# Activations in alternating 64-byte pieces for a float32r transformer kernel on one core

## The chip, the cores and the metric

The kernel runs on one core of one Trainium2 chip. The metric is the device time of one execution in microseconds (us), the median of several executions. A difference of 0.2% (3.5 us) is about what a measurement of this kernel can tell from no change.

## The reference, cut to what matters

Ten sublayers work on one sequence of 256 tokens with 1024 channels. Each normalizes the residual stream, scales and shifts it by values computed from a conditioning vector, runs a mixer or a feed-forward network, and adds the result back through a gate:

```
def modulate(x, g, c_act, w, b):
    m = c_act @ w + b
    shift, scale, gate = jnp.split(m, 3, axis=-1)
    h = rmsnorm(x, g) * (1.0 + scale[:, None, :]) + shift[:, None, :]
    return h, gate[:, None, :]

def swiglu(h, w_gate, w_up, w_down):
    return (jax.nn.silu(h @ w_gate) * (h @ w_up)) @ w_down
```

In the order of the kernel the sublayers are: feed-forward, Mamba-2 mixer, feed-forward, feed-forward, block attention ("moba"), feed-forward, stick-breaking attention ("sb"), convolutional feed-forward, sparse latent attention ("dsa"), convolutional feed-forward. The feed-forward width is 2816. Everything is float32.

## The kernel before, in words

**Layout.** Activations lie transposed: channels on the 128 partitions, the 256 tokens (T) along the free axis. The normalized input of a stage is eight such tiles (KT = 8, index kk).

**Three products for one.** Float32 accuracy comes from float32r products (F32R). Every operand is split into a high part (a rounded copy, made by ScalarE) and a low part (the rest, made by VectorE as original minus copy). `three` (lines 1573 to 1577) then issues hi x hi, hi x lo and lo x hi, each a 128x128 stationary weight tile under a 128x256 moving activation tile. Weights come in 276 blocks of 128x2048, one megabyte each, by SP's queue into `raw` (six buffers). ScalarE writes `w_hi` (line 496), VectorE `w_lo` (line 915), three buffers each, two blocks ahead of TensorE (AHEAD = 2). One block is 48 products.

**Activations.** `norm` builds a stage's input. VectorE writes the scaled tiles (`t`, line 1036), ScalarE adds the shift and rounds into `h_hi` (line 530), VectorE writes the low part (line 1043). TensorE's first block of a stage (`gemm` with `first`) takes the tiles as they come: 32 products with `h_hi` (lines 1588, 1591), then 16 with the low parts (line 1602), each pair waiting for its tile. Later blocks of a stage run over kk = 0 to 7 for each half of the block. The products of a feed-forward's down projection and of the mixers' output projections (`gemm_out`, `last`, `early_out`) read `a_hi` and `a_lo`, which ScalarE (lines 555, 603, 684, 749) and VectorE (lines 1120, 1176, 1293, 1414) write once per group. In the attention stages some blocks ("tokens") have it the other way about: activations stationary and weights moving.

**Addresses.** `h_hi` lies 1472 bytes behind a multiple of 8192 bytes from the weight buffers (x, `folded3`, `gs` between them), `h_lo_rest` (tiles 1 to 7) directly behind it, so both begin 192 bytes past a multiple of 256 from the weights. Tile 0 of the low part has a buffer of its own, `h_lo_first`, 64 bytes further on, a multiple of 256 from the weights. For kk = 0 the low product is issued first (lines 1632 to 1634, in place of `three`).

```
        h_hi = sb("h_hi", [P, KT, T], F32R)
        h_lo_rest = sb("h_lo_rest", [P, KT - 1, T], F32R)
        gap = sb("gap", [P, 16])
        h_lo_first = sb("h_lo_first", [P, T], F32R)
        gap2 = sb("gap2", [P, 48])
```

**Order.** Each engine runs its own list in order; semaphores tie them. VectorE's list carries side work too: in stages 0, 2, 3, 5 and 7 it accumulates the modulation vectors of later stages (line 970, from `modws`), spread over the iterations by a table. In a stage's `norm` it stands as eight `t`, eight low parts, then the rest of a weight split (`late_split`). During a `norm` TensorE runs filler products on the first weight block (`fill`, line 1697), moving and stationary operand both from `w_hi`.

## Time and profile before

| | |
|---|---|
| median of 3 runs | 1773.77 us (1773.60 to 1774.51) |
| the profiled execution | 1783.76 us, span 1782.0 us |
| TensorE matmul busy | 1742.4 us (98%), 14686 products |
| VectorE busy | 1452.5 us (82%) |
| ScalarE busy | 956.5 us (54%) |
| mean granted TensorE clock | 0.998 of full speed |

Matmuls are pipelined, so that one recorded product overlaps the next two. The busy share says little; the distance from start to start is what a product costs. It is read from the timeline or as a window's length over its count.

### The profile page before, as it was taken

Reading aid. Unit: us, or ns where it says so; the run is one execution under the profiler, and the core shown is the slowest. Engines: PE = TensorE matmul, PEld = TensorE weight load, DVE = VectorE, ACT = ScalarE, POOL = GpSimd, SP = SyncE. Lnnn points to the kernel's source line nnn. Section 1 sums busy time; section 2 is a strip of 40 time slices with the busy share of each in tenths; the row PEclk is TensorE's granted clock in tenths of the full one; section 3 lists DMA queues with packets and bytes.
Section 4 is the critical chain, followed back from the end, with each engine's and each line's share of the span. In section 5 each row is a group of like instructions: output and inputs, shape, how many; then the busy total and the mean of one; then the engine's idle time right before and its main releaser. Section 6 shows DMA issues by size and latency. Waiting matters only on the chain.

```text
span 1782.0 us, 34261 instructions
## 1 busy us (share of the span) xinstructions
PE 1742.4 (98%) x14686; PEld 1699.3 (95%) x14686; DVE 1452.5 (82%) x1750; ACT 956.5 (54%) x1254; POOL 0.2 (0%) x4
## 2 busy tenths in 40 slices
PE   5999999999999999999999999999999999999999
PEld 4999999998999999999999999999999998989999
DVE  7799899988898879897558989765899888567776
ACT  4444566676533454445765333566655556675553
POOL 0000000000000000000000000000000000000000
PEclk9999999999999999999999999999999999999999
DMA  9999734443798859895436988343387545316550
GB/s 395 411 420 332 308 143 166 166 144 141 313 394 328 331 204 389 326 379 183 149 141 227 387 309 352 147 154 124 127 302 282 210 147 187 141 72 218 186 199 34
DMA packets 68149, 426.23 MB, mean 239 GB/s; under 512 B 7488, under 2 KB 10832, under 8 KB 31824
## 3 DMA queue, kind: packets, MB, share of 16 engines
q1 hardware_dynamic: 63936, 416.22, 61.3%
q10 hardware_dynamic: 4112, 8.62, 1.4%
q8 instruction: 68, 1.11, 0.3%
q14 instruction: 33, 0.27, 0.0%
HBM read 423.74 MB, written 3.17 MB: 240 GB/s over the span
## 4 chain that ended last, share of the span: by engine, by line
PE 93%; DVE 3%; ACT 3%; DMA 1%; issue 0%; DVEq 0%; SPq 0%; ACTq 0%
PE bank L1575 25%; PE bank L1576 24%; PE bank L1577 24%; PE bank L1632 2%; PE bank L1634 2%; PE bank L1633 2%; PE bank L1588 1%; PE bank L1688 1%; PE bank L1602 1%; PE bank L1991 1%; DMA mix<-mods 1%; PE bank L1591 1%; ACT w_hi L496 1%; PE bank L1859 1%; ACT work L719 0%; PE bank L1972 0%
## 5 line engine op out<-in xcount | busy, mean ns | idle before, releaser
L1575 PE MATMUL bank<-h_hi,w_hi 128*128 128x256 f32 x2504 | 696.2, 278 | 0.0
L1577 PE MATMUL bank<-h_hi,w_lo 128*128 128x256 f32 x2504 | 695.2, 278 | 0.0
L1576 PE MATMUL bank<-h_lo_rest,w_hi 128*128 128x256 f32 x2504 | 695.2, 278 | 0.0
L915 DVE TENSOR_TENSOR w_lo<-raw,w_hi 128x2048 fp32r<-128x2048 f32 x267 | 609.5, 2284 | 91.4 <-ACT w_hi L496 90.4
L496 ACT ACTIVATE w_hi<-raw 128x2048 fp32r<-128x2048 f32 x276 | 527.9, 1913 | 159.7 <-PE bank L1577 146.1
L1575 PEld LDWEIGHTS bank<-h_hi,w_hi 128*128 128x128 f32 x2504 | 473.0, 189 | 0.0
L1576 PEld LDWEIGHTS bank<-h_lo_rest,w_hi 128*128 128x128 f32 x2504 | 470.2, 188 | 0.0
L1577 PEld LDWEIGHTS bank<-h_hi,w_lo 128*128 128x128 f32 x2504 | 470.1, 188 | 0.0
L1575 PE MATMUL bank<-a_hi,w_hi 128*128 128x256 f32 x1280 | 358.6, 280 | 0.8 <-DVE a_lo L1293 0.8
L1577 PE MATMUL bank<-a_hi,w_lo 128*128 128x256 f32 x1280 | 355.4, 278 | 0.0
L1576 PE MATMUL bank<-a_lo,w_hi 128*128 128x256 f32 x1280 | 355.4, 278 | 0.0
L1575 PEld LDWEIGHTS bank<-a_hi,w_hi 128*128 128x128 f32 x1280 | 241.9, 189 | 3.1 <-issue 1.4
L1576 PEld LDWEIGHTS bank<-a_lo,w_hi 128*128 128x128 f32 x1280 | 240.4, 188 | 0.1
L1577 PEld LDWEIGHTS bank<-a_hi,w_lo 128*128 128x128 f32 x1280 | 240.4, 188 | 0.0
L970 DVE SCALAR_TENSOR_TENSOR macc<-modws,cact,macc 128x1536 f32<-128x1536 f32 x126 | 225.8, 1811 | 1.2 <-DMA modws<-mods 1.2
L1156 DVE SCALAR_TENSOR_TENSOR mix<-bank,par,mix 128x254 f32<-128x254 f32 (+1 forms) x176 | 76.7, 477 | 41.3 <-ACT mix L582 39.8
L1632 PE MATMUL bank<-h_lo_first,w_hi 128*128 128x256 f32 x344 | 100.2, 291 | 1.6 <-DVE work L1378 1.4
L555 ACT ACTIVATE a_hi<-mix 128x512 fp32r<-128x512 f32 x40 | 25.3, 633 | 141.0 <-PE bank L1577 125.5
L1634 PE MATMUL bank<-h_hi,w_lo 128*128 128x256 f32 x344 | 97.8, 284 | 0.0
L1633 PE MATMUL bank<-h_hi,w_hi 128*128 128x256 f32 x344 | 96.6, 281 | 0.0
L582 ACT ACTIVATE mix<-bank,par 128x256 f32<-128x256 f32 x88 | 44.9, 561 | 91.8 <-PE bank L1577 91.8
L541 ACT ACTIVATE mix<-bank 128x512 f32<-128x512 f32 x44 | 26.4, 600 | 117.8 <-PE bank L1577 117.7
(304 smaller groups left out, 1986.3 us busy)
## 6 DMA issues: line engine op xcount, KB each, us to landing
raw<-weights SPq DMA_DIRECT2D x276, 1024.0 KB, 5.3
modws<-mods SPq DMA_DIRECT2D x144, 768.0 KB, 6.7
mix<-mods SPq DMA_DIRECT2D x5, 1024.0 KB, 8.8
mix<-mods ACTq DMA_DIRECT2D x8, 512.0 KB, 13.3
biases<-scratch ACTq DMA_DIRECT2D x1, 2048.0 KB, 13.3
mix<-biases ACTq DMA_DIRECT2D x4, 512.0 KB, 3.8
modws<-mods SPq DMA_DIRECT2D x1, 1024.0 KB, 11.6
x<-xin SPq DMA_DIRECT2D x1, 1024.0 KB, 10.9
```

Of the source, the lines that this page charges most:

```text
L496: eng.activation(w_hi[g % NW][:, :], raw[g % NRAW][:, :], ACT.Copy).then_inc(sems["whi"], 1)
L541: k.inc("silu", eng.activation(sg, bank[4][:, :].rearrange("p (a t) -> p a t", a=2), ACT.Silu))
L582: ins = eng.activation(dst[:, m, :], b[:, m * T:(m + 1) * T], ACT.Identity, scale=cw(i, t, 2), bias=cw(i, t, 3))
L915: eng.tensor_tensor(w_lo[g % NW][:, :], raw[g % NRAW][:, :], w_hi[g % NW][:, :], ALU.subtract).then_inc(sems["wlo"], 1)
L970: ins = eng.scalar_tensor_tensor(out=m, in0=modw[q % 4], scalar=c, in1=m, op0=ALU.mult, op1=ALU.add)
L1156: ins = eng.scalar_tensor_tensor(out=dst[:, m, lag:T], in0=b[:, m * T:(m + 1) * T - lag], scalar=cw(i, 22 * up + m, tap), in1=dst[:, m, la ...
L1575: eng.matmul(dst, ah, bh, start=start, stop=False, skip_group_check=skip)
L1576: eng.matmul(dst, ah, bl, start=False, stop=False, skip_group_check=skip)
L1577: return eng.matmul(dst, al, bh, start=False, stop=stop, skip_group_check=skip)
L1632: eng.matmul(d, hi[:, kk, part], h_lo(kk), start=True, stop=False)
L1633: eng.matmul(d, hi[:, kk, part], h_hi[:, kk, :], start=False, stop=False)
L1634: eng.matmul(d, lo[:, kk, part], h_hi[:, kk, :], start=False, stop=False)
```

## The change

`h_hi`, `h_lo_all` (all eight low tiles in one buffer), `a_hi` and `a_lo` now begin 128 bytes past a multiple of 256 bytes from the weight buffers, by gaps of other sizes. `h_lo_first` and the low-product-first order for kk = 0 are gone; `three` serves all kk. Except for `h` in the stages moba and sb, a tile of 256 tokens is stored as two halves of 512 bytes: tokens 0 to 15 in the first, 16 to 31 in the second, 32 to 47 in the first, and so on. The moving operand of each product is an access pattern that takes 64 bytes (16 tokens) from one half, then 64 from the other, so that the product sees the tokens in order. ScalarE writes `h_hi` in this order by one instruction with a longer pattern. The writes of `a_hi` on ScalarE and of all low parts on VectorE become two instructions each, one per half. In moba and sb `h` is stored in token order, since blocks there use it as the stationary operand.

```diff
+        gap = sb("gap", [P, 48])
         h_hi = sb("h_hi", [P, KT, T], F32R)
-        h_lo_rest = sb("h_lo_rest", [P, KT - 1, T], F32R)
-        gap = sb("gap", [P, 16])
-        h_lo_first = sb("h_lo_first", [P, T], F32R)
-        gap2 = sb("gap2", [P, 48])
+        h_lo_all = sb("h_lo_all", [P, KT, T], F32R)
+        gap2 = sb("gap2", [P, 16])
+        def by_chunks(tile):
+            return tile.rearrange("p (e j q) -> p j e q", e=2, q=16)
+        def in_order(tile):
+            return tile.rearrange("p (j e q) -> p j e q", e=2, q=16)
+        def chunked(st):
+            return stages[st] not in ("moba", "sb")
+        def h_lo(n, st):
+            return by_chunks(h_lo_all[:, n, :]) if chunked(st) else in_order(h_lo_all[:, n, :])
+        def hh(n, st):
+            return by_chunks(h_hi[:, n, :]) if chunked(st) else in_order(h_hi[:, n, :])
...
+        gap3 = sb("gap3", [P, 48])
         a_hi = sb("a_hi", [P, 2, T], F32R)
         a_lo = sb("a_lo", [P, 2, T], F32R)
+        def halves(tiles, e):
+            return tiles[:, :, e * P:(e + 1) * P].rearrange("p a (j q) -> p a j q", q=16)
+        def halves_in_order(tiles, e):
+            return tiles.rearrange("p a (j e q) -> p a j e q", e=2, q=16)[:, :, :, e]
...
-                    k.inc("hhi", eng.activation(h_hi[:, m, :], work3[:, m, :], ACT.Identity,
+                    k.inc("hhi", eng.activation(hh(m, st), in_order(work3[:, m, :]), ACT.Identity,
                                                 bias=modv[:, st, m:m + 1]))
...
-                    k.inc("ahi", eng.activation(z_hi if final else a_hi[:, :, :], act, ACT.Copy))
+                    to = z_hi if final else a_hi
+                    for e in range(2):
+                        ins = eng.activation(halves(to, e), halves_in_order(act, e), ACT.Copy)
+                    k.inc("ahi", ins)
...
-                    k.inc("hlo", eng.scalar_tensor_tensor(
-                        out=h_lo(m), in0=work3[:, m, :], scalar=modv[:, st, m:m + 1],
-                        in1=h_hi[:, m, :], op0=ALU.add, op1=ALU.subtract))
+                    for e in range(2):
+                        ins = eng.scalar_tensor_tensor(
+                            out=h_lo(m, st)[:, :, e], in0=in_order(work3[:, m, :])[:, :, e], scalar=modv[:, st, m:m + 1],
+                            in1=hh(m, st)[:, :, e], op0=ALU.add, op1=ALU.subtract)
+                    k.inc("hlo", ins)
...
-                    k.inc("alo", eng.tensor_tensor(z_lo if final else a_lo[:, :, :], act,
-                                                   z_hi if final else a_hi[:, :, :], ALU.subtract))
+                    to, other = (z_lo, z_hi) if final else (a_lo, a_hi)
+                    for e in range(2):
+                        ins = eng.tensor_tensor(halves(to, e), halves_in_order(act, e), halves(other, e), ALU.subtract)
+                    k.inc("alo", ins)
...
-                            elif kk == 0:
-                                eng.matmul(d, hi[:, kk, part], h_lo(kk), start=True, stop=False)
-                                eng.matmul(d, hi[:, kk, part], h_hi[:, kk, :], start=False, stop=False)
-                                eng.matmul(d, lo[:, kk, part], h_hi[:, kk, :], start=False, stop=False)
                             else:
-                                mm = three(d, hi[:, kk, part], lo[:, kk, part], h_hi[:, kk, :], h_lo(kk),
+                                mm = three(d, hi[:, kk, part], lo[:, kk, part], hh(kk, st), h_lo(kk, st),
                                            kk == 0, kk == KT - 1)
...
-                        mm = three(acc(m), hi[:, kk, part], lo[:, kk, part], a_hi[:, kk, :], a_lo[:, kk, :],
+                        mm = three(acc(m), hi[:, kk, part], lo[:, kk, part], by_chunks(a_hi[:, kk, :]), by_chunks(a_lo[:, kk, :]),
                                    fresh and kk == m % 2 == 0, False, True)
```

The other places of the diff repeat these forms.

TensorE's list where the second block of the first feed-forward ends and the third begins, with kk = 0 and 1, before:

```order
L1615 MATMUL bank<-h_hi,w_lo 128x256 x16
L1632 MATMUL bank<-h_lo_first,w_hi 128x256
L1633 MATMUL bank<-h_hi,w_hi 128x256
L1634 MATMUL bank<-h_hi,w_lo 128x256
L1575 MATMUL bank<-h_hi,w_hi 128x256
L1576 MATMUL bank<-h_lo_rest,w_hi 128x256
```

The same place in the changed kernel:

```order
L1661 MATMUL bank<-h_hi,w_lo 128x256 x16
L1621 MATMUL bank<-h_hi,w_hi 128x256
L1622 MATMUL bank<-h_lo_all,w_hi 128x256
L1623 MATMUL bank<-h_hi,w_lo 128x256
L1621 MATMUL bank<-h_hi,w_hi 128x256
L1622 MATMUL bank<-h_lo_all,w_hi 128x256
```

The number of products is the same; for kk = 0 the high product comes first now, as for every other kk.

VectorE's list around the `norm` of the first stage and the first group of its feed-forward, before:

```order
L1036 SCALAR_TENSOR_TENSOR work<-x,gs,rstd 128x256 x8
L929 TENSOR_TENSOR w_lo<-raw,w_hi 128x1024
L1043 SCALAR_TENSOR_TENSOR h_lo_first<-work,modv,h_hi 128x256
L1043 SCALAR_TENSOR_TENSOR h_lo_rest<-work,modv,h_hi 128x256 x7
L915 TENSOR_TENSOR w_lo<-raw,w_hi 128x2048 x3
L1114 TENSOR_TENSOR mix<-mix,bank 128x512
L1120 TENSOR_TENSOR a_lo<-mix,a_hi 128x512
```

The same stretch of VectorE's list in the changed kernel:

```order
L1071 SCALAR_TENSOR_TENSOR work<-x,gs,rstd 128x256 x8
L964 TENSOR_TENSOR w_lo<-raw,w_hi 128x1024
L1079 SCALAR_TENSOR_TENSOR h_lo_all<-work,modv,h_hi 128x128 x16
L950 TENSOR_TENSOR w_lo<-raw,w_hi 128x2048 x3
L1151 TENSOR_TENSOR mix<-mix,bank 128x512
L1159 TENSOR_TENSOR a_lo<-mix,a_hi 128x2x128 x2
```

Nothing changes places. The eight low parts are sixteen instructions of half the length, and the group's `a_lo` is two.

## Rows read from the trace of the kernel before

**Rows 1.** The page's busy times of each engine, with instruction counts.

```profile
PE 1742.4 (98%) x14686; PEld 1699.3 (95%) x14686; DVE 1452.5 (82%) x1750; ACT 956.5 (54%) x1254; POOL 0.2 (0%) x4
```

**Rows 2.** The page's chain that ended last, shares by engine.

```profile
PE 93%; DVE 3%; ACT 3%; DMA 1%; issue 0%; DVEq 0%; SPq 0%; ACTq 0%
```

**Rows 3.** Windows inside stages 0, 1, 2, 3, 5, 7, 9; columns in first row.

```profile
core 0: us, PE busy (x) PEld busy (x) DVE busy (x) ACT busy (x) POOL busy (x), PEclk, DMA share, GB/s
80.00:200.00 120.00, 120.00 (x1054) 120.00 (x1053) 116.21 (x76) 49.55 (x37) 0.00 (x0) 1.00 0.97 383
230.00:440.00 210.00, 207.24 (x1759) 198.14 (x1758) 188.22 (x289) 139.34 (x188) 0.00 (x0) 1.00 0.43 159
460.00:620.00 160.00, 160.00 (x1361) 160.00 (x1360) 140.99 (x88) 64.30 (x49) 0.00 (x0) 1.00 0.92 366
650.00:810.00 160.00, 160.00 (x1405) 160.00 (x1404) 144.25 (x90) 65.80 (x49) 0.00 (x0) 1.00 0.91 356
...
955.00:1115.00 160.00, 160.00 (x1361) 160.00 (x1360) 140.88 (x88) 65.38 (x49) 0.00 (x0) 1.00 0.89 345
...
1275.00:1435.00 160.00, 160.00 (x1405) 160.00 (x1404) 146.10 (x155) 86.61 (x91) 0.00 (x0) 1.00 0.71 256
...
1610.00:1770.00 160.00, 160.00 (x1405) 160.00 (x1405) 115.26 (x133) 85.45 (x89) 0.00 (x0) 1.00 0.44 158
```

**Rows 4.** TensorE's timeline at a change of tile 0, stage 0: start us, duration us.

```profile
150.32 0.28 PE L1575 MATMUL bank<-h_hi,w_hi 128*128 128x256 f32 x1
...
150.55 0.28 PE L1577 MATMUL bank<-h_hi,w_lo 128*128 128x256 f32 x1
150.66 0.28 PE L1632 MATMUL bank<-h_lo_first,w_hi 128*128 128x256 f32 x1
150.78 0.28 PE L1633 MATMUL bank<-h_hi,w_hi 128*128 128x256 f32 x1
150.90 0.29 PE L1634 MATMUL bank<-h_hi,w_lo 128*128 128x256 f32 x1
151.03 0.28 PE L1575 MATMUL bank<-h_hi,w_hi 128*128 128x256 f32 x1
```

**Rows 5.** Line 1575, durations min/median/max: weights stationary, then weights moving.

```profile
L1575 PE MATMUL bank<-h_hi,w_hi x2504: 276/276/367, 46.4 to 1778.2; 128*128 128x256 f32 x193
...
L1575 PE MATMUL bank<-w_hi,h_hi x112: 278/280/280, 838.2 to 1240.0; 128*128 128x256 f32 x112
```

**Rows 6.** Timeline of filler products, then of six transposes of 128 columns.

```profile
824.74 1.47 PE L1697 MATMUL bank<-w_hi 128*128 128x256 f32 x11
...
851.00 0.82 PE L1972 MATMUL bank<-con,work 128*128 128x128 f32 x6
```

**Rows 7.** Line 1972 (transposes), durations min/median/max.

```profile
L1972 PE MATMUL bank<-con,work x96: 270/272/330, 851.0 to 1583.1; 128*128 128x128 f32 x96
```

**Rows 8.** VectorE and TensorE, timeline at the start of stage 4.

```profile
828.72 0.48 DVE L1043 SCALAR_TENSOR_TENSOR h_lo_first<-work,modv,h_hi 128x256 fp32r<-128x256 f32 x1
829.12 2.85 DVE L1043 SCALAR_TENSOR_TENSOR h_lo_rest<-work,modv,h_hi 128x256 fp32r<-128x256 f32 x7
...
830.68 1.85 PE L1602 MATMUL bank<-h_lo_rest,w_hi 128*128 128x256 f32 x14
832.36 0.28 PE L1632 MATMUL bank<-h_lo_first,w_hi 128*128 128x256 f32 x1
```

**Rows 9.** Groups by shape: VectorE's low parts, a half-length form; busy us, mean ns.

```profile
L1120 DVE TENSOR_TENSOR a_lo<-mix,a_hi 128x512 fp32r<-128x512 f32 x40 | 27.6, 690 | 30.6 <-ACT a_hi L555 30.4
L1414 DVE TENSOR_TENSOR a_lo<-bank,a_hi 128x256 fp32r<-128x256 f32 x24 | 10.1, 422 | 43.2 <-ACT a_hi L749 43.2
L1378 DVE SCALAR_TENSOR_TENSOR work<-bank,mix,modws 128x128 f32<-128x128 f32 x12 | 4.0, 338 | 0.3 <-ACT mix L502 0.3
```

**Rows 10.** VectorE and TensorE, timeline at the start of stage 0.

```profile
36.52 2.85 DVE L1043 SCALAR_TENSOR_TENSOR h_lo_rest<-work,modv,h_hi 128x256 fp32r<-128x256 f32 x7
...
38.88 1.81 PE L1602 MATMUL bank<-h_lo_rest,w_hi 128*128 128x256 f32 x14
```

More of the change, by code:

```diff
@@ L748, in out_hi @@
                     b = bank[5 if kind == "dsa" else 4]
-                    k.inc("ahi", eng.activation(a_hi[:, p, :], b[:, p * T:(p + 1) * T], ACT.Copy))
+                    for e in range(2):
+                        ins = eng.activation(by_chunks(a_hi[:, p, :])[:, :, e], in_order(b[:, p * T:(p + 1) * T])[:, :, e],
+                                             ACT.Copy)
+                    k.inc("ahi", ins)
                 def latent(i, p):
@@ L1175, in lo @@
                     k.wait("ahi", st, i, 1, 0)
-                    k.inc("alo", eng.tensor_tensor(z_lo if final else a_lo[:, :, :], act,
-                                                   z_hi if final else a_hi[:, :, :], ALU.subtract))
+                    to, other = (z_lo, z_hi) if final else (a_lo, a_hi)
+                    for e in range(2):
+                        ins = eng.tensor_tensor(halves(to, e), halves_in_order(act, e), halves(other, e), ALU.subtract)
+                    k.inc("alo", ins)
                 def down(i, a, b):
@@ L1292, in lo @@
                     k.wait("ahi", st, i, 1, -1)
-                    k.inc("alo", eng.tensor_tensor(a_lo[:, :, :], yn, a_hi[:, :, :], ALU.subtract))
+                    for e in range(2):
+                        ins = eng.tensor_tensor(halves(a_lo, e), halves_in_order(yn, e), halves(a_hi, e), ALU.subtract)
+                    k.inc("alo", ins)
                 def group_rows(i):
@@ L1413, in out_lo @@
                     b = bank[5 if kind == "dsa" else 4]
-                    k.inc("alo", eng.tensor_tensor(a_lo[:, p, :], b[:, p * T:(p + 1) * T], a_hi[:, p, :],
-                                                   ALU.subtract))
+                    for e in range(2):
+                        ins = eng.tensor_tensor(by_chunks(a_lo[:, p, :])[:, :, e],
+                                                in_order(b[:, p * T:(p + 1) * T])[:, :, e],
+                                                by_chunks(a_hi[:, p, :])[:, :, e], ALU.subtract)
+                    k.inc("alo", ins)
                 def mask_bias(i):
@@ L1596, in gemm @@
                         for m, part, d in both:
-                            eng.matmul(d, lo[:, kk, part], h_hi[:, kk, :], start=False, stop=False,
+                            eng.matmul(d, lo[:, kk, part], hh(kk, st), start=False, stop=False,
                                        skip_group_check=True)
@@ L1601, in gemm @@
                         for m, part, d in both:
-                            mm = eng.matmul(d, hi[:, kk, part], h_lo(kk), start=False, stop=kk == KT - 1,
+                            mm = eng.matmul(d, hi[:, kk, part], h_lo(kk, st), start=False, stop=kk == KT - 1,
                                             skip_group_check=True)
@@ L1607, in gemm @@
                         for m, part, d in both:
[L1608 removed]
+                            eng.matmul(d, hi[:, kk, part], h_lo(kk, st), start=kk == m == 0, stop=False,
                                        skip_group_check=True)
[L1610 removed]
+                            eng.matmul(d, hi[:, kk, part], hh(kk, st), start=False, stop=False,
                                        skip_group_check=True)
@@ L1614, in gemm @@
                         for m, part, d in both:
-                            mm = eng.matmul(d, lo[:, kk, part], h_hi[:, kk, :], start=False, stop=kk == KT - 1,
+                            mm = eng.matmul(d, lo[:, kk, part], hh(kk, st), start=False, stop=kk == KT - 1,
                                             skip_group_check=True)
@@ L1746, in early_out @@
                     part = slice(m * P, (m + 1) * P)
-                    three(acc(m), hi[:, 0, part], lo[:, 0, part], a_hi[:, 0, :], a_lo[:, 0, :], False, False, True)
+                    three(acc(m), hi[:, 0, part], lo[:, 0, part], by_chunks(a_hi[:, 0, :]), by_chunks(a_lo[:, 0, :]), False, False, True)
             def last(st, ready, early=0, token_squares=None):
@@ L1772, in last @@
                     for kk in range(1 if m < early else 0, 2):
-                        mm = three(acc(m), hi[:, kk, part], lo[:, kk, part], ahi[:, kk, :], alo[:, kk, :],
+                        mm = three(acc(m), hi[:, kk, part], lo[:, kk, part], by_chunks(ahi[:, kk, :]), by_chunks(alo[:, kk, :]),
                                    False, False, True)
```

31 lines of the change are left out of this document (14 added, 17 removed).

## The prediction

> **What bounds the kernel now.** I read the page's busy times first: TensorE is busy 98% of the span, VectorE 82%, ScalarE 54% [rows 1]. The chain that ended last runs through TensorE for 93% [rows 2]. So almost the whole time is TensorE's own pace, and the question is what one product costs, not who waits for whom. The windows answer it [rows 3]. Each lies inside a stage, TensorE is never idle in those of the feed-forward stages, the granted clock is 1.00 (the 2.4 GHz level), and all the work there is 128x256 float32r products. The counts include the two or three products that only overlap an edge. Stages 3, 7 and 9 have 160 us over about 1402, **114.1 ns** from start to start; stage 0 has 120 over about 1051, the same. Stages 2 and 5 have 160 over about 1359, **117.7 ns**. The instructions are the same in kind and number, VectorE and ScalarE are no busier there than in 3 and 7, and nobody waits. At 2.4 GHz, 256 columns are 106.7 ns. So 7 to 11 ns of every product are something else.
>
> What the something is shows in the rows at tile 0. The three steps before it take 0.34 us, 0.113 each; with `h_lo_first`, which lies at another distance from the weights, they become 0.12, 0.12 and 0.13 us, and TensorE waited for no one [rows 4]. Shape, line and engine are the same; only the address differs. Recorded durations say the same in another way: 276 ns in the common case with weights stationary, 280 with weights moving and activations stationary, so at yet another distance [rows 5]. The filler products, whose two operands come from the same tile, follow each other at (1.47 - 0.28)/10 = 119 ns [rows 6]. I read this as the moving read and the weight read of the next product meeting in the same part of SBUF once or more in each product, a few ns each time. The moving read covers 1024 bytes in the time in which the weight read covers 512, so in token order it overtakes the weights' read, wherever it starts. An offset can only change how often they meet (114.1 or 117.7 ns), never make it zero.
>
> **The change part by part.** *The reading order.* With 64 bytes from one half and then 64 from the other, 512 bytes on, the moving read advances, modulo 512 (and so modulo 256 or 128), only 64 bytes while the weight read advances 64. The two go in step. They start 128 bytes apart modulo 256 and stay there to within 32 bytes. If a meeting costs time, there should be none left. No row shows a float32r product of 256 columns without meetings. The nearest is the transposes, 128 columns of f32: (0.82 - 0.27)/5 = 110 ns apart [rows 6], with a median duration of 272 ns against 276 [rows 5, 7]; their two reads have the same length. The lower end is 106.7 ns, 256 columns at the granted clock; the upper end is that the pieces themselves cost something, up to the 117.7 of the worse stages or beyond. I take **109 ns**, nearest to the transposes.
>
> The products that change: stages 3, 7 and 9 have 33 blocks x 48 = 1584 each, 3 x 1584 x (114.1 - 109) = 24.2 us. Stage 0: 1584 x 5.1 = 8.1. Stages 2 and 5: 2 x 1584 x 8.7 = 27.6. Stage 1 has 32 x 48 = 1536 and stage 8 has 15 x 48 = 720; these mix both paces, and I take the middle, 115.5: 2256 x 6.5 = 14.7. The output projections of stages 4 and 6 are 8 x 48 = 384: 2.5. Sum **77 us**. The 24 other blocks of stages 4 and 6 stay in token order at a new offset: 1152 products x up to 2.2 ns either way, 2.5 us, taken as zero.
>
> *The low parts at a stage's start.* This is the cost that isn't hidden. VectorE is done with the eight low tiles at 829.12 + 2.85 = 831.97, one each 0.395 us (2.85 - 0.48 over 6) [rows 8]. TensorE starts its last 14 low products at 830.68 and the next block at 832.36; its last pair, at about 832.1, starts some 0.15 us after the last low tile is done. There is no slack. One instruction of this kind takes 0.48 us [rows 8] and one of half its length 0.34 [rows 9], 0.14 shorter, so the pair takes 2 x (0.395 - 0.14) = 0.51 us. Each tile adds 0.12 us to the delay, the eight together 1.0 us. TensorE, quicker in the 48 products of this block, only waits longer: 0.2 us of the gain above isn't got. That is 1.2 us in nine stages. In stage 0 the last low tile is done at 39.37 and its pair starts at about 40.3 [rows 10], which leaves 0.3: **11 us**.
>
> *The two-piece writes elsewhere.* On VectorE an `a_lo` of 128x512 takes 690 ns and one of 128x256 422 [rows 9], so the split adds about 0.15 us to each of 68, and as much to each of 24 smaller ones: 14 us in all, on an engine with room. In a feed-forward stage it is 11 x 0.15 = 1.7 us. ScalarE adds about as much at 54% busy. Where nothing waits for these, they cost nothing. The cover is TensorE's lead: VectorE is at 88 to 91% in stages 2, 3, 5 and 7 [rows 3]. There TensorE's 160 us become 148 to 153, VectorE's 141 to 146 plus 1.5 fill 95 to 97% of them: tight, still below. Stage 0 is over the edge: 116.2 of 120 us busy. TensorE would need 120 x 109/114.1 = 114.6 us for the same work, VectorE 116.2 + 1.2 = 117.4. That is 2.8 in this window, and I give **2.5 us** back. Stage 1 has VectorE at 90% and TensorE with 2.8 us idle in 210: its chains of small steps don't shrink with the products. **3 us** back. The handoffs at the ends of mixers (a high and a low part, in a row, before the last projection) are longer by some 0.3 us at a dozen places, part of them hidden: **2 us**.
>
> *No special tile.* Removing `h_lo_first` removes the 0.12 and 0.13 us steps [rows 4]; that is in the 114.1 already.
>
> Sum: 77 - 11 - 2.5 - 3 - 2 = 58 us. The profiled execution took 1783.8 us, 10 us over the median shown; it becomes 1726, and the median **1716 us**, 3.3% faster.
>
> **The rivals.** *A: one meeting stays.* The pieces bring all stages to the better pace and no further, 113.3 ns, the 0.11 us steps of a long even stretch (340 ns for three). For it: the window rows know two paces only, and the better one may be the floor of such products. Then 6336 products gain 0.8 ns, 3168 gain 4.4, 2640 gain 2.2: 25 us, less 14.5 us of costs (the 11 at the starts, 3.5 of stage 1 and the handoffs; VectorE doesn't bind in stage 0): 1764 us.
>
> *B: the reads don't meet at all.* The pace has some other cause, the new order leaves it where it is, and only these 14.5 us of costs remain, above all the low parts at the stage starts. That is 1788 us, **slower**. It decides when the saving per product is under 14.5 us / 12144 = 1.2 ns. Against it: rows 4, where nothing but an address changed. The Trainium skill speaks for it: "SBUF — State Buffer", section "Who interferes with whom", lists two independent read ports for the array's moving operand and its weights and says that PE never waits on anyone. By that rule the pace couldn't depend on where buffers lie, and this change would be B. The trace disagrees with it, by 114.1 against 117.7 ns and by the steps at tile 0.
>
> *C: the pieces slow the moving read*, since each product now makes 16 jumps. At 117.7 ns everywhere 6336 products lose 3.6 ns and 2640 lose 2.2: 29 us, and 14.5 of costs: 1817 us. Nothing in the profile has such a moving operand, so nothing speaks against it but that ScalarE and VectorE read strided tiles at their usual pace.
>
> **How the numbers follow.** Forecast 64%, its own range 1698 to 1736: from 107.5 ns per product to 110.7. A 14%, B 12%, C 10%. The range reaches from the forecast's low end over A, 1698 to 1768; B and C, 22%, are out. Within 0.2% (3.5 us, about what a measurement tells) lies only the space between A and B, 4%. Faster 76%, slower 20%.
>
> **What would show it.** Windows in the feed-forward stages should count some 1465 products in 160 us, the same in stages 2 and 3, at a median duration of about 272 ns. TensorE should wait for VectorE at each stage's start by about 1.2 us, on the line of the low products. VectorE should be busy 25 to 30 us more, and in stage 0 TensorE should show waits for `w_lo`. The prediction is wrong in its core if stages 2 and 3 still differ, or if the count stays at or under 1405.

## The result, and the profile after

| | before | after |
|---|---|---|
| median | 1773.68 us (1773.49 to 1774.51) | 1850.05 us (1849.44 to 1850.61) |
| the profiled execution | 1783.76 us, span 1782.0 | 1849.44 us, span 1847.7 |

The change makes the kernel **4.2% slower**: the ratio is 1.0419 [1.0403, 1.0436]. The forecast was 3.3% faster, 1716 us, with a range up to 1768.

First the page of the changed kernel: busy times, then the chain that ended last, by engine.

```profile
PE 1809.4 (98%) x14686; PEld 1761.4 (95%) x14686; DVE 1472.4 (80%) x1928; ACT 964.4 (52%) x1352; POOL 0.2 (0%) x4
...
PE 95%; ACT 2%; DVE 2%; DMA 1%; issue 0%; DVEq 0%; SPq 0%; ACTq 0%
```

Against [rows 1] and [rows 2] the count of products is the same, 14686, and TensorE holds still more of the chain. VectorE has grown by 20 us and its share of the span has fallen. So no other engine took over as the bound: each product has become dearer. The windows show it, each inside the same stage as its row in [rows 3].

```profile
core 0: us, PE busy (x) PEld busy (x) DVE busy (x) ACT busy (x) POOL busy (x), PEclk, DMA share, GB/s
80.00:200.00 120.00, 120.00 (x1002) 120.00 (x1001) 111.15 (x77) 48.13 (x42) 0.00 (x0) 1.00 0.91 362
240.00:450.00 210.00, 208.07 (x1711) 199.19 (x1710) 184.49 (x282) 135.94 (x189) 0.00 (x0) 1.00 0.43 157
475.00:635.00 160.00, 160.00 (x1336) 160.00 (x1335) 138.35 (x95) 62.88 (x58) 0.00 (x0) 1.00 0.92 366
672.00:832.00 160.00, 160.00 (x1336) 160.00 (x1335) 138.42 (x97) 63.89 (x57) 0.00 (x0) 1.00 0.89 343
990.00:1150.00 160.00, 160.00 (x1336) 160.00 (x1335) 139.03 (x97) 64.26 (x57) 0.00 (x0) 1.00 0.89 343
1320.00:1480.00 160.00, 160.00 (x1335) 160.00 (x1334) 140.25 (x154) 82.64 (x96) 0.00 (x0) 1.00 0.69 246
1665.00:1825.00 160.00, 160.00 (x1335) 160.00 (x1334) 110.86 (x135) 82.81 (x95) 0.00 (x0) 1.00 0.45 162
```

160 us over 1333 products (1335 or 1336 less the two or three that overlap an edge) are **120.0 ns** in every feed-forward stage, and 120 over 1000 in stage 0. Before it was 114.1 or 117.7 ns, and 109 was forecast. The clock is 1.00 in all of them, and TensorE is never idle. The spread between stages is gone, but at a pace worse than both. The durations agree; these two rows are line 1621, the same three products as before's line 1575, with minimum, median and maximum, first for weights stationary, then for weights moving.

```profile
L1621 PE MATMUL bank<-h_hi,w_hi x2848: 274/282/472, 46.1 to 1843.8; 128*128 128x256 f32 x190
...
L1621 PE MATMUL bank<-w_hi,h_hi x128: 274/281/369, 870.0 to 1282.4; 128*128 128x256 f32 x128
```

276 ns in [rows 5] has become 282. The first row reads its moving operand in pieces. The second doesn't: there the weights move, in token order. It went from 280 to 281 only.

The start of stage 4 answers to [rows 8]: start, duration, engine and line.

```profile
857.60 0.36 PE L1634 MATMUL bank<-h_hi,w_hi 128*128 128x256 f32 x1 [0.50 <-ACT h_hi L554]
...
859.60 4.29 DVE L1079 SCALAR_TENSOR_TENSOR h_lo_all<-work,modv,h_hi 128x128 fp32r<-128x128 f32 x16
...
861.47 2.97 PE L1648 MATMUL bank<-h_lo_all,w_hi 128*128 128x256 f32 x16
864.28 0.28 PE L1621 MATMUL bank<-h_hi,w_hi 128*128 128x256 f32 x1
```

Sixteen half tiles take 4.29 us where eight whole ones took 3.25 (828.72 to 831.97). The sixteen low products are spread over 2.81 us, 176 ns each, since they follow the tiles. From the first product of the stage to its next block it is 6.68 us. Before, that first product was this one, and the block began at 832.36 [rows 8]: 5.64 us.

```profile
826.72 0.36 PE L1588 MATMUL bank<-h_hi,w_hi 128*128 128x256 f32 x1 [0.51 <-ACT h_hi L530]
```

That is 1.04 us a stage, about what was forecast (1.0 for the tiles, 1.2 with TensorE's longer wait). It is a small part of 76 us.

### The profile page after: what moved, and what is told of

Read it like the earlier page. It is cut to its first block, busy times and chain, and to the rows that moved or that the text cites. A ratio compares the mean times of both kernels' runs of the same rounds, so it can differ in the third digit from the quotient of the medians.

```text
span 1847.7 us, 34537 instructions
## 1 busy us (share of the span) xinstructions
PE 1809.4 (98%) x14686; PEld 1761.4 (95%) x14686; DVE 1472.4 (80%) x1928; ACT 964.4 (52%) x1352; POOL 0.2 (0%) x4
## 4 chain that ended last, share of the span: by engine, by line
PE 95%; ACT 2%; DVE 2%; DMA 1%; issue 0%; DVEq 0%; SPq 0%; ACTq 0%
PE bank L1621 28%; PE bank L1623 27%; PE bank L1622 27%; PE bank L1648 1%; PE bank L1634 1%; PE bank L1726 1%; PE bank L2029 1%; DMA mix<-mods 1%; PE bank L1637 1%; PE bank L2010 0%; PE bank L1897 0%; PE bank L2001 0%; PE bank L2030 0%; PE bank L1948 0%; PE bank L1982 0%
## 5 line engine op out<-in xcount | busy, mean ns | idle before, releaser
L1621 PE MATMUL bank<-h_hi,w_hi 128*128 128x256 f32 x2848 | 807.6, 284 | 1.5 <-DVE work L1421 1.3
L1623 PE MATMUL bank<-h_hi,w_lo 128*128 128x256 f32 x2848 | 803.9, 282 | 0.0
L1622 PE MATMUL bank<-h_lo_all,w_hi 128*128 128x256 f32 x2848 | 803.8, 282 | 0.0
L1621 PEld LDWEIGHTS bank<-h_hi,w_hi 128*128 128x128 f32 x2848 | 535.3, 188 | 5.1 <-issue 2.2
L1622 PEld LDWEIGHTS bank<-h_lo_all,w_hi 128*128 128x128 f32 x2848 | 535.3, 188 | 0.0
L1623 PEld LDWEIGHTS bank<-h_hi,w_lo 128*128 128x128 f32 x2848 | 535.3, 188 | 0.0
L581 ACT ACTIVATE a_hi<-mix 128x256 fp32r<-128x256 f32 x80 | 29.0, 409 | 148.7 <-PE bank L1623 132.2
L565 ACT ACTIVATE mix<-bank 128x512 f32<-128x512 f32 x44 | 26.4, 601 | 126.6 <-PE bank L1623 123.3
L1159 DVE TENSOR_TENSOR a_lo<-mix,a_hi 128x256 fp32r<-128x256 f32 x80 | 30.4, 422 | 42.8 <-ACT a_hi L581 42.8
L792 ACT ACTIVATE mix<-bank 128x512 f32<-128x512 f32 x32 | 19.0, 595 | 64.9 <-PE bank L1623 60.0
L1151 DVE TENSOR_TENSOR mix<-mix,bank 128x512 f32<-128x512 f32 x44 | 30.3, 688 | 26.9 <-PE bank L1623 26.8
```

The lines of the kernel that those rows point to most:

```text
L565: k.inc("silu", eng.activation(sg, bank[4][:, :].rearrange("p (a t) -> p a t", a=2), ACT.Silu))
L581: ins = eng.activation(halves(to, e), halves_in_order(act, e), ACT.Copy)
L1151: k.inc("mul", eng.tensor_tensor(act, sg, bank[5][:, :].rearrange("p (a t) -> p a t", a=2), ALU.mult))
L1159: ins = eng.tensor_tensor(halves(to, e), halves_in_order(act, e), halves(other, e), ALU.subtract)
L1621: eng.matmul(dst, ah, bh, start=start, stop=False, skip_group_check=skip)
L1622: eng.matmul(dst, ah, bl, start=False, stop=False, skip_group_check=skip)
```

## The experiments

**What one product costs by itself.** `ladder1` computes nothing of the reference: it is sections of 96 products of 128x256 float32r from a buffer with weights and a buffer with moving data. From section to section only the moving operand changes: its distance from the weights modulo 512 bytes, and the order in which it is read.

```
for i in range(96):
    k = i % 8
    eng.matmul(bank[:, 0:256], w[:, 256*k : 256*k+128], pattern(mv, 256*k + offset), start=True, stop=True)
```

> The kernel does none of the reference's work: it only issues 34 sections of 96 float32r products (stationary 128x128, moving 128x256), alternately from two weight buffers, with the moving operand at different distances from the weights and in different patterns (in sequence; 4, 8, 16, 32 or 64 columns from alternate halves; halves further apart; in sequence with gaps). Theory J (each jump of the moving pattern costs a fixed time, about 13 ns over 16 pieces, 0.8 ns each): 64-byte pieces 120 ns at every offset and every distance of the halves; 128-byte pieces 114 or less, 256-byte pieces less again; 32-byte pieces 133; 64-byte pieces in sequence with gaps 120 too. Theory M (the lockstep pieces meet the weight read because 128 bytes is the wrong distance): 64-byte pieces fall to about 109 ns at some other offset and reach 120 or more at others; halves 576 or 640 bytes apart change the pace; gaps cost nothing by themselves. In sequence both expect 113 to 120 ns by offset.

Its timeline has one row per section: start, length. A product's pace is the length less the last product's own 0.28 us, over 95. The rows are token order at 128, 192 and 256 bytes, then pieces of 16 columns (64 bytes, as in the change) at 128 and 192 bytes, and at 128 bytes pieces of 4, 8 and 64 columns.

```profile
63.54 11.56 PE L72 MATMUL bank<-mv,wa 128*128 128x256 f32 x96
...
86.20 11.07 PE L72 MATMUL bank<-mv,wa 128*128 128x256 f32 x96
...
108.46 11.68 PE L72 MATMUL bank<-mv,wa 128*128 128x256 f32 x96
...
165.93 11.69 PE L72 MATMUL bank<-mv,wb 128*128 128x256 f32 x96
177.45 11.68 PE L72 MATMUL bank<-mv,wa 128*128 128x256 f32 x96
...
212.01 12.58 PE L72 MATMUL bank<-mv,wb 128*128 128x256 f32 x96
224.43 12.00 PE L72 MATMUL bank<-mv,wa 128*128 128x256 f32 x96
...
247.79 11.55 PE L72 MATMUL bank<-mv,wa 128*128 128x256 f32 x96
```

In token order the distance decides: 118.7 ns at 128 bytes, 120.0 at 0, 96 and 256, 117.4 to 118.6 at five others, and **113.3 ns at 192** alone (113.6 by the row, which has dearer first steps in it; the last ten are at 113.3 to 113.4). In 64-byte pieces it is **120.0 ns at all seven distances tried**. Shorter pieces cost more: 123.3 ns with 8 columns, 129.4 with 4. So 120.0 ns is the pace of the changed kernel, with no VectorE, DMA or wait in it. Theory M lost: no distance and no other spacing of the halves brought the pieces below 120.0 ns. Theory J kept its 120 ns but not its price per jump: with pieces of 32 columns, half the jumps, it was 120.0 ns too, and with pieces of 8 columns 123.3 where it had expected 133. What a jump costs stays open.

**The change with its reading order undone.** `order_only` keeps the two-part writes and all distances of the changed kernel, and stores and reads in token order.

```diff
-            return tile.rearrange("p (e j q) -> p j e q", e=2, q=16)
+            return tile.rearrange("p (j e q) -> p j e q", e=2, q=16)
```

> The changed kernel with its buffers and two-piece writes, but every tile stored and read in token order. Theory J: the products fall back to the pace of token order at 128 bytes, 118.7 ns as in the attention stages of the changed kernel, so about 1835 us. Theory M: the same, since token order doesn't go in step; this run gives the share of the offset and of the special tile (about 4.5 ns on some 9500 products, 43 us) and of the two-piece writes (14 to 17 us) against the share of the pieces (some 15 us).

```profile
672.00:832.00 160.00, 160.00 (x1351) 1.00 0.89 342
```

It took 1834.83 us (1834.22 to 1835.58), ratio 1.0343 [1.0325, 1.0360]. The row, which has TensorE's figures alone, is stage 3: 160 over 1348, 118.7 ns, the value of `ladder1` at 128 bytes. So the pieces account for 15.2 us of the 76, and 61 us come from what stayed.

**The change at before's distance.** `pieces_at192` has the pieces, and the buffers 192 bytes from the weights.

```diff
-        gap = sb("gap", [P, 48])
-        gap2 = sb("gap2", [P, 16])
+        gap2 = sb("gap2", [P, 64])
```

> The changed kernel with its pieces, but buffers 192 bytes past a multiple of 256 from the weights, as before the change. Theory J: 120.0 ns per product as at 128, 1850 us. Theory M: another pace, between 109 and 125 ns, so under 1740 or over 1870 us, unless 192 is as bad as 128.

The cut leaves out `gap3`, which moves `a_hi` and `a_lo` by the same 64 bytes. It took 1847.6 us, in a single execution, its windows again at 1335 or 1336. Read in pieces, a product costs 120.0 ns here as there. What the pieces cost depends on what they replace: 1.3 ns a product at 128 bytes, 6.7 at 192.

**Does the pace keep?** `ladder2` is more sections of the same kind. 

> Again none of the reference's work, 33 sections of 96 products. The first ladder gave 120.0 ns for 64-byte pieces at seven distances, 113.3 ns in sequence at 192 bytes and 117 to 120 elsewhere, and more jumps did not cost in proportion (32 jumps 123, 64 jumps 129). Theory W (the weight read is what suffers: it is slower whenever a moving read is at hand, so that in step it suffers all along): with 64 or 32 stationary columns every pattern falls to about 107 to 110 ns, jumps included; a moving operand of 512 columns takes 213 to 216 ns; weights read with every second column, so as fast in bytes as a moving operand in sequence, are in step without a jump and show 120 or an offset with 109. Theory J2 (the moving pattern itself is slow, 4-dimensional or jumping): 64-byte pieces stay at 120 ns with 32 stationary columns, and 512 columns in pieces take some 13 to 27 ns more than in sequence. In sequence at 192 bytes, 113.3 ns whatever went before would say that the pace has no memory; 117.7 after another pattern would say that it has.

Three of its rows: token order at 192 bytes, after a section at 0; pieces at 192; and token order at 192 once more, right after the pieces.

```profile
28.45 11.06 PE L98 MATMUL bank<-mv,wb 128*128 128x256 f32 x96
...
50.23 11.70 PE L98 MATMUL bank<-mv,wb 128*128 128x256 f32 x96
61.76 11.47 PE L98 MATMUL bank<-mv,wa 128*128 128x256 f32 x96
```

Products of the same kind, at the same distance, ran 96 times at 113.3 ns and 96 times at 117.8. The weights lay in the other of the two weight buffers here; the pairs of `ladder3` below show both paces with the very same addresses. So the pace is a rhythm that keeps itself up, and what ran before chooses it. Distances of 176, 184, 200 and 208 bytes gave 119 to 120 ns, so 192 is a narrow place. 448 bytes gave 113.3. Theory W failed: with 64 or 32 stationary columns no pattern fell to 107 to 110 ns, and pieces of 16 columns stayed at 120.0. Other results of this run: a second PSUM bank in turn changes nothing; 512 columns take 226.7 ns in token order at distance 0 but 233.3 at 192, and 240.0 in pieces. The good distance for 256 columns isn't the good one for 512.

**Before, without its special tile.** `plain192` is the kernel before with one buffer at 192 bytes for all eight low tiles, and the order of the three products of tile 0 as for the others.

```diff
-        h_lo_rest = sb("h_lo_rest", [P, KT - 1, T], F32R)
-        gap = sb("gap", [P, 16])
-        h_lo_first = sb("h_lo_first", [P, T], F32R)
-        gap2 = sb("gap2", [P, 48])
+        h_lo_all = sb("h_lo_all", [P, KT, T], F32R)
+        gap2 = sb("gap2", [P, 64])
```

> The kernel before with the special tile undone: all eight low tiles in one buffer at 192 bytes, high product first for kk = 0 too; one-piece writes, token order. If the offset of 192 bytes alone sets the good pace (113.3 ns), the dear steps around tile 0 go and the time is 1774 us or some 10 us less. If the pace has a memory and the special tile is what brings it back to the good state, most stages run at 117.7 ns: about 12000 products by 3 ns, 1800 to 1810 us.

1795.16 us, ratio 1.0130 [1.0113, 1.0147], and it scatters, 1785.04, 1792.62, 1797.70, 1798.92, where seven executions of the kernel before measured beside it lay between 1772.70 and 1773.94. Stages 3, 5 and 7 of the one at 1785, TensorE alone:

```profile
645.00:805.00 160.00, 160.00 (x1414) 1.00 0.91 354
955.00:1115.00 160.00, 160.00 (x1362) 1.00 0.88 344
1275.00:1435.00 160.00, 160.00 (x1361) 1.00 0.68 243
```

Stages 0, 2 and 3 ran at 113.4 ns, stages 5, 7 and 9 at 117.7. These are the two rhythms of `ladder2`, now in the kernel. The tile that the prediction costed at nothing, with its order, is worth 22 us in the median of these four.

**The floor and the way back.** `ladder3` reads the same moving operands with one stationary column, so that hardly anything is read for the weights, and tries what leads from the worse rhythm to the better. 

> None of the reference's work; three groups of sections. (1) With one stationary column, so that almost no weights are read. Theory R (the moving read pays by itself for its pieces): 64-byte pieces stay near 120 ns, and token order is near 107 to 109. Theory W (only weights and moving read together are slow): every pattern near 107 to 109. (2) In sequence at 192 bytes 113.3 ns after a run at distance 0; patterns of 2, 4, 8, 16 pieces at 192 bytes then show what the first jumps cost. Theory R: a rise with the pieces, 0.8 ns each: 115, 117, 120, up to 120 or more at 16. If a single jump already gives the full 120 ns, the good pace of 113.3 is a state that any disturbance ends, and the count of jumps does not matter. (3) After 64-byte pieces, 24 products in sequence at 192 bytes run at 117.7 ns, the worse pace; then a few disturbing products, then 60 more. At least one of the disturbances (some products at distance 0, or one short product) brings back 113.3; one more ordinary product does not.

One stationary column: token order at 192, 0 and 128 bytes, pieces of 16 columns, pieces of 4 columns. Then pairs of rows. The first of each ends in token order at 192 in the worse rhythm and then one ordinary product (x41), or two at distance 0 (x42); the second is 60 products more at 192.

```profile
22.22 11.05 PE L84 MATMUL bank<-mv,wa 128*1 128x256 f32 x96
33.11 11.06 PE L84 MATMUL bank<-mv,wb 128*1 128x256 f32 x96
44.01 11.07 PE L84 MATMUL bank<-mv,wa 128*1 128x256 f32 x96
54.91 11.68 PE L84 MATMUL bank<-mv,wb 128*1 128x256 f32 x96
...
89.47 12.16 PE L84 MATMUL bank<-mv,wa 128*1 128x256 f32 x96
...
243.31 5.03 PE L84 MATMUL bank<-mv,wa 128*128 128x256 f32 x41
248.18 7.23 PE L84 MATMUL bank<-mv,wb 128*128 128x256 f32 x60
...
267.18 5.15 PE L84 MATMUL bank<-mv,wa 128*128 128x256 f32 x42
272.17 6.97 PE L84 MATMUL bank<-mv,wb 128*128 128x256 f32 x60
```

This separates the two causes. With one column for the weights token order ran at 113.3 ns at all three distances. So what 0 and 128 bytes cost more in token order, 120.0 and 118.7 ns, comes with reading the weights' many columns. And 113.3 is the least that any section of float32r products of 256 columns held in these runs, not 109. But the pieces cost 120.0 ns with one column as well, at 0 and at 192 bytes: that loss is the moving read's own, and none of the distances tried took it away. Nor is it the number of jumps: a single gap of 64 bytes in the middle of the 256 columns gave 120.0, while pieces of 64 columns, three jumps, ran at 113.3 at 192 bytes with 128 stationary columns. Why some jumps cost and others don't, no run shows.

The pairs: after one ordinary product the 60 stay at (7.23 - 0.28)/59 = 117.8 ns, after two at distance 0 they are at 113.4. One at distance 0 left them at 117.8. One or two products of 128 columns led back as well; a single one of 16 or 64 columns didn't.

**The distance alone, and the writes.** `plain128` is `plain192` with buffers at 128 bytes.

```diff
+        gap = sb("gap", [P, 48])
-        gap2 = sb("gap2", [P, 64])
+        gap2 = sb("gap2", [P, 16])
```

> The kernel before with the special tile undone and all activation buffers at 128 bytes, one-piece writes, token order. Against the run at 192 bytes (1795 us) it gives the share of the offset: products at 118.7 ns in place of 113.3 or 117.7, so about 12900 x 3.3 ns = 40 us, 1825 us. Against the run in token order with two-piece writes (1835 us) it gives the share of these writes, 10 to 14 us by the prediction's term of 11. If the offset is innocent, it stays at 1795 to 1800 us.

```profile
665.00:825.00 160.00, 160.00 (x1350) 1.00 0.89 343
```

1825.2 us (1824.13 to 1825.93), 118.7 ns in all feed-forward stages: against the median of `plain192` 64 bytes of distance cost 30 us, and since its four executions lie 14 us apart, this 30 is as loose as the 22 of the tile. The sum of both, 52 us, doesn't hang on them. `order_only` is this kernel with writes in two parts, 1834.8: they cost 9.6 us.

`two_lows` is the kernel before with only the low tiles of h written in two halves.

```diff
+                    for e in range(2):
+                        cc = slice(e * P, (e + 1) * P)
+                        ins = eng.scalar_tensor_tensor(out=h_lo(m)[:, cc], in0=work3[:, m, cc], ...
```

> The kernel before with one change: each of the eight low tiles at a stage's start is written by two VectorE instructions of 128 columns. By the prediction's term (TensorE waits for the last low tile) 10 to 11 us slower, 1784 us. If there is hidden slack, under 3 us.

```profile
460.00:620.00 160.00, 160.00 (x1405) 1.00 0.93 377
...
955.00:1115.00 160.00, 160.00 (x1405) 1.00 0.90 353
```

1783.93 us, ratio 1.0045 [1.0030, 1.0059]. The ten executions of the kernel before measured beside it stood in two groups, three at 1773.0 to 1773.6 and seven at 1777.9 to 1779.6. The rows say why they can. They are stages 2 and 5, at 114.1 ns; in the profiled execution of before, at 1783.8, these two were at 117.7 [rows 3]. By that difference a stage of 1584 products in the worse rhythm is 5.7 us longer. So the profile on which the prediction was built had two such stages, and an execution at 1773 should have none; that is worked out, since only one execution of before has a trace. It also means that executions of before differ by more than the 0.2% given for a measurement. Against 1773.3 the halves cost 10.6 us, against the median of all ten, 1778.0, only 5.9. The trace speaks for the first: all six big stages of this execution are at the better pace, and stage 4 of `two_lows` takes 6.70 us from its first product to its next block (824.64 to 831.34) where before took 5.64. Ten stages at 1.06 us are 10.6, and 11 us were forecast for the starts.

**Setting the rhythm.** `reset192` is `plain192` with one product in each of 11 blocks issued as two of 128 columns.

```diff
+  elif (m == kk == 1 and stages[st] in ("ffn", "cffn") and isinstance(i, int)
+        and (i, b) in ((0, 1), (1, -1))):
+      for half in (slice(0, P), slice(P, T)):
+          eng.matmul(d[:, half], hi[:, kk, part], h_hi[:, kk, half], start=False, ...
```

> The changed kernel with token order, writes in one piece and buffers 192 bytes from the weights (as in plain192), and in two places of each of the seven big stages one 256-column product is issued as two of 128 columns. Theory of a kept state (the pace at 192 bytes has two values, 113.3 ns and 117.8 ns, and short products bring back the first): all seven stages run at 113.3 to 113.5 ns, the time is 1760 to 1768 us, below the kernel before, and does not scatter from run to run. Rival (the state is set by something else that differs between stages, and two short products do not set it): some stages stay at 117.6 to 117.8 ns, and the time is 1785 to 1799 us as plain192 had it. Third: the short products' own cost, 14 pairs at some 10 ns, is under 1 us in either case.

(The big stages are six, not seven, and in stage 0 only one block is split: 11 places.)

```profile
955.00:1115.00 160.00, 160.00 (x1412) 1.00 0.90 354
...
1275.00:1435.00 160.00, 160.00 (x1410) 1.00 0.71 255
```

**1769.77 us (1768.26 to 1775.46, 12 runs), ratio 0.9967 [0.9949, 0.9985]**: faster than the kernel before by 0.3%, and than the changed one by 80 us. Stages 5 and 7, at 1362 and 1361 in `plain192`, count 1412 and 1410: 113.5 to 113.7 ns. With 11 products more, 25 us less than `plain192`. The time is 2 us above the expected range, and one of twelve runs was still 6 us off.

`ladder4` asks what leads out of the better rhythm. 

> Chains of products alone, no reference work. A stretch at 192 bytes follows either a good stretch or one of pieces, with a short disturbance between. Theory of a kept state: the state that 64-byte pieces leave (117.8 ns) is left again after 2 or more products at 0 bytes or after short products, and a single disturbance in the good state leaves 113.3 ns except where it is a product in pieces, which brings 117.8 ns. Rival (the pace depends on the count of products before, not on a state): the stretch after one product in pieces differs from the stretch after none by nothing, 113.3 ns both. At 448 bytes the same values. With one stationary column: pieces of 2, 4, 8, 16 columns 130, 125, 120, 120 ns, of 32 and 64 columns 117 to 118 ns, one gap in the middle of 8 columns 120 ns, of 128 columns 120 ns; token order 113.3 ns beside every one of them.

A stretch in the better rhythm, then one product at distance 0 (x71 in all) or two (x72), then 60 at 192 bytes:

```profile
22.31 8.50 PE L84 MATMUL bank<-mv,wa 128*128 128x256 f32 x71
30.65 6.98 PE L84 MATMUL bank<-mv,wb 128*128 128x256 f32 x60
37.47 8.59 PE L84 MATMUL bank<-mv,wa 128*128 128x256 f32 x72
45.90 7.23 PE L84 MATMUL bank<-mv,wb 128*128 128x256 f32 x60
```

Half of this expectation failed. After one product at 0 it stays at 113.4, after two it falls to 117.8, after three or eight it is good again; one product in pieces left it good, and one short product of 16 columns brought 117.8. From the worse rhythm, at 448 bytes, two or eight at 0 led out and one or three didn't. So these runs give no rule of good and bad disturbances; that the moment at which the steady stretch begins decides is a guess. Two products of 128 columns ended in the better rhythm each time, from either side. With 32 stationary columns 0 and 64 bytes gave 113.3 ns and 192 gave 116.7, so the good distance depends also on how much is loaded (at 0 it was 117.8 in `ladder2`: there too it can be either). With one stationary column the expected 113.3 ns in token order beside every pattern failed too. Four of ten stretches of 20 products at 192 bytes ran at 116.7 ns, as the first of these two, after pieces of 16 columns, (2.50 - 0.28)/19:

```profile
481.58 2.50 PE L84 MATMUL bank<-mv,wb 128*1 128x256 f32 x20
...
509.33 2.43 PE L84 MATMUL bank<-mv,wb 128*1 128x256 f32 x20
```

So the second rhythm doesn't need many columns of weights.

**More of the same.** `split_all` splits one product in every input block, 172 in all. 

> As reset192, but one product is issued as two of 128 columns in every block of the input products, the mixers' blocks among them. Theory of a kept state that short products set: the steps of the big stages that reset192 still showed at 115 to 119 ns (57 to 177 of some 1600 in a stage) and those of the mixers (302 to 543 of 733 to 1563) go to 113.3 ns, which gives 1 us in the big stages and up to 5 us in the mixers, less some 90 splits at about 5 to 10 ns each, under 1 us: 1763 to 1768 us. Rival (the mixers' steps at 115 to 119 ns are where other products come between, and no state that a split sets): 1769 to 1771 us, the same as reset192.

```profile
49.70 0.33 PE L1627 MATMUL bank<-h_hi,w_hi 128*128 128x128 f32 x2
49.88 0.33 PE L1629 MATMUL bank<-h_lo_all,w_hi 128*128 128x256 f32 x1
50.05 0.28 PE L1631 MATMUL bank<-h_hi,w_lo 128*128 128x256 f32 x1
50.16 0.28 PE L1573 MATMUL bank<-h_hi,w_hi 128*128 128x256 f32 x1
```

A miss: 1786.87 us, ratio 1.0062 [1.0046, 1.0077]. I had counted some 90 splits, and priced one at 5 to 10 ns. By the timeline of one, from 49.70 to 50.16, three products' worth take 0.46 us in place of 0.34: a split costs about 117 ns, as much as one product more. 172 of them are 20 us; without them it would be 1767 by this estimate, so what the rhythm gives in the mixers is some 2 us at most.

`pieces64` puts the split and the good distance under the change itself, with pieces of 64 columns (256 bytes).

```diff
-            return tile.rearrange("p (e j q) -> p j e q", e=2, q=16)
+            return tile.rearrange("p (e j q) -> p j e q", e=2, q=64)
```

> The changed kernel with pieces of 256 bytes (64 columns) in place of 64 bytes, buffers 192 bytes from the weights, and the two split products of each big stage. If what a product in pieces costs comes from how short the piece is (alone, pieces of 64 columns at 192 bytes ran at 113.3 ns, pieces of 16 at 120.0 ns): the big stages run at 113.3 to 114.5 ns, and the time is that of reset192, 1770 us, and some 10 us for writes in two parts, 1778 to 1784 us. If any order from alternate halves costs it: 120.0 ns, 1845 to 1850 us. Between, if the pieces leave the state at 117.7 ns in spite of the splits: 1800 to 1825 us.

```profile
650.00:810.00 160.00, 160.00 (x1414) 1.00 0.90 353
```

1778.23 us (1777.01 to 1783.43), ratio 1.0018 [1.0007, 1.0030]: 113.3 ns, where the same kernel with 16 columns a piece and no splits has 120.0 and 1847.6 us. Two things differ from `pieces_at192`, the length of the pieces and the splits, and they weren't tried apart. The 8 us over `reset192` fit the 9.6 measured for writes in two parts.

## Why the prediction was wrong

**The step that failed is the reading order**: "The two go in step", "If a meeting costs time, there should be none left", "I take **109 ns**". Measured were 120.0. Two things in it were wrong. The floor: no stretch of 256-column products went below 113.3 ns, with or without weights to read. The transposes' 110 ns for 128 columns were the nearest row, but the split shows that a short product is paced by something else (112 ns for the second half). And the pieces' own cost: 6.7 ns a product over that floor, at all seven distances tried, even with one stationary column. The term was forecast at 77 us of gain; with 120.0 ns in its place the same products lose 57 us.

**The idea of a meeting of reads** fits token order in part: at 0, 128 and 192 bytes the pace differs with 128 stationary columns (120.0, 118.7, 113.3 ns) and not with one (113.3). That the reads meet is not shown by it, and it was no argument for the pieces. Nor could it explain 114.1 against 117.7 ns, as the prediction had it, by "how often they meet": those stages have the same distance, and differ in rhythm. The new distance of 128 bytes, taken as "zero" for the token-order blocks and thought indifferent for the others, costs some 30 us in token order.

**"No special tile", costed at nothing**, hid the largest surprise. I read the 0.12 and 0.13 us steps at tile 0 [rows 4] as a loss by address alone. But two of the three dear products there have their usual distance. `ladder4` has the same steps without any such tile: one product at distance 0 in a good stretch is followed by steps of 119, 119, 124 and 118 ns, then 113, and in stage 3 of before most passages of tile 0 show just these. So they are what a disturbance costs until the rhythm is back. They are the 0.7 ns between 114.1 and the 113.4 of `plain192`, by estimate 7 us in six stages. Yet without that tile and its order the kernel takes 22 us more and scatters, and with 11 split products instead it takes 4 us less.

That the tile would reset the rhythm each time it comes by is not so. This row of before is from the window of stage 2, which ran at 117.7 ns:

```profile
L1632 PE MATMUL bank<-h_lo_first,w_hi 128*128 128x256 f32 x39 | 11.0, 283 | 0.0
```

The tile passed 39 times, and the stage stayed in the worse rhythm; in stage 3 it passed as often and the better one stayed. In the traces of before and of `plain192` a big stage keeps to its end the rhythm it has soon after its start. So the tile or its order must act there, on how often a stage begins well: all six stages in a usual execution of before, three of six in the profiled one of `plain192`. How is open; the two weren't tried apart.

**Two stages of the profile** (2 and 5, 117.7 ns) were read as how the kernel runs. It was that one execution: 10 us over the median, which the prediction had noted and carried along without asking where they came from. So of the 27.6 us for these stages 2 x 1584 x 3.6 ns = 11 us weren't to be had in a usual execution.

**The costs** held in the main. The starts: 11 us forecast, 10.6 measured. VectorE was to be 25 to 30 us busier, and is 20. The 3 us of stage 1 and the 2 of the handoffs no run separates; all writes in two parts together cost 9.6 us at 128 bytes, so little is left for them. That VectorE would bind in stage 0 didn't come up, since TensorE became slower and VectorE's share fell from 116.2 to 111.2 of 120 us.

**The rivals.** C, "the pieces slow the moving read", had the mechanism. Its price, 117.7 ns, was the worse of the two paces in [rows 3], though the filler products showed 119 [rows 6]; with 120.0 the same sum gives 57 us against the profiled execution (6336 products at 5.9 ns, 3168 at 2.3, 2640 at 4.5), about 4 for the token-order blocks at 118.7, 10 for the starts. That is 71, where 65.7 were measured. The 5 us over may be steps in which TensorE had waited anyway; no run shows it. B's size of a loss was too small, and A's floor of 113.3 ns was right. The Trainium skill, "SBUF — State Buffer", section "Who interferes with whom", by which PE never waits on anyone, was held to be refuted by the trace. `ladder1` agrees with the trace for token order, 113.3 to 120.0 ns by distance, and so does the kernel, 118.7 ns at 128 bytes. The rule had not spoken for this change either way, since what the pieces cost stays with one stationary column.

**The sum as measured**, each step from one run to the next, before, `plain192`, `plain128`, `order_only`, changed kernel: special tile and its order 22 us, distance 30, two-part writes 10, pieces 15: 77, and 76.4 in all. The parts depend on their order: at 192 bytes the pieces alone already bring 120.0 ns, and `pieces_at192` is within 3 us of the changed kernel.

## What to carry to other kernels

When TensorE is never idle and its pace stands some per cent over the columns' own time, measure that pace in a kernel of nothing but such products, for the distances and patterns in question, before changing hundreds of instructions; one run of 34 sections would have decided this case. A moving operand that isn't contiguous can cost by itself: here 64-byte pieces add 6.7 ns to 113.3, and 256-byte pieces nothing at 192 bytes. And where a profiled execution stands off the median, find the stage that makes the difference before building on its rows.

## What the runs showed of the hardware that I had not expected

- Same instructions, same addresses, two paces: 113.3 and 117.8 ns a product, each kept for as long as the stretch lasts (60 products in `ladder3`, a whole stage in the kernel), chosen by what ran just before. In the kernel this is 5 to 6 us a stage.
- Of all distances tried in token order with 128 stationary and 256 moving columns only 192 and 448 bytes gave 113.3 ns; 8 bytes off, at 184 or 200, it was 120.0.
- With one stationary column: 113.3 ns contiguous (116.7 in some short stretches), 120.0 in pieces of 16 columns, 125.0 in pieces of 4, 120.0 with a single gap of 64 bytes.
- One product at distance 0 within a stretch at 192 bytes left the rhythm as it was, the better and the worse. In the better one it cost four dearer steps, 119, 119, 124 and 118 ns.
- Two products of 128 columns cost 117 ns more than the one of 256 they replace.
